# Small norms in a fused five-block kernel: the inverse root moved from ScalarE and VectorE to GpSimd

## The chip, the cores and the metric

The kernel runs on one NeuronCore of one Trainium2 chip. The core has four compute engines with their own instruction queues, which work in parallel and meet only at semaphores: TensorE (PE in the profile; its weight loads are PEld), VectorE (DVE), ScalarE (ACT) and GpSimd (POOL). SyncE (SP) issues most DMA transfers. The metric is the time of one execution on the device, in microseconds (us), as the median of several executions.

## The reference, cut to what matters

A sequence of 256 tokens with 1024 features runs through two layers of one model (a mixer of gated delta rule and mLSTM, then attention with a window; feed-forward parts after each) and two layers of a second one (a mixer of five kinds of attention, then a gated feed-forward part). Everything is float32. Between the large products stand many norms over few numbers, all of this form:

```python
def _rms_norm(x, g):
    xf = x.astype(jnp.float32)
    y = xf * lax.rsqrt(jnp.mean(xf * xf, axis=-1, keepdims=True) + EPS)
    return (y * g.astype(jnp.float32)).astype(x.dtype)

def l2norm(x):
    return x * lax.rsqrt(jnp.sum(x * x, -1, keepdims=True) + EPS)
```

The heads of queries and keys are normed by it one by one, so one norm of 8 heads for 256 tokens has 16 means on each of 128 partitions, and 2 to 32 in the other cases.

## The kernel before

The weights come as float32 and are used as a sum of two halves: for every part of 128x1024 numbers ScalarE writes `weights_high` (L663), VectorE writes `weights_low`, the rest (L765), and TensorE multiplies three times (L490 to L492). Both engines do this for all weights of the kernel, some parts ahead of TensorE, and everything else of theirs is put between by hand: each engine's program is one list in the order in which the code is written (`scalar_program`, `vector_program` and so on), and each instruction waits for the semaphore counts that it needs. A later instruction of an engine never overtakes one that waits.

A small norm went through four engines' queues. GpSimd squares (in the mixer of the second model L2552), VectorE sums (L2378), scales and adds epsilon, and signals `mean` (L2387, L2384, L2480); ScalarE takes the root in place (`scalar_root`, L695) and signals `root`; VectorE takes the reciprocal in place (`vector_inverse`, L784), signals `inverse` and goes on with the product (L2393). There are 21 such roots: one each for the first norm of the input ("ab", tile `inv`), for the l2 norms of the delta rule ("ab l2", L1173), for the two outputs of the first mixer (`ss_b`, `ss_a`) and for the memory (`mem_inv`), and eight in each of the two second-model layers, tile `st`: "memk", "cq", "fox", "mla", "moba", "diff", "memq" and "sub".

The mixer of the second model, `mixer_2`, first projects (2916 columns), with "memk", "cq", "fox" and "mla" between the projections, and then runs six groups of heads through a loop in five stages that are shifted against each other (`skewed`): heads turned into `QK`, scores into `S`, row maximum `mx` and exponentials (L1939), turned probabilities `PT`, values. "moba", "diff" and "memq" prepare the groups 2, 3 and 5 from within that loop, and "sub" norms the output of group 4. ScalarE's place for each root in its list is behind the exponentials of the group before:

```python
    def work(n):
        if n == 2:
            roots("moba", 11, 8)
        elif n == 3:
            roots("diff", 19, 16)
        elif n == 5:
            roots("memq", 35, 4)
```

ScalarE has one table of functions loaded at a time. Where the next function isn't in it, the compiler puts an ACT_TABLE_LOAD ahead of the instruction. Root and exponential are in different tables here; copy, cast and square cause no load. The wide norms over 1024 features (`scalar_sums_root`, L736, with the reciprocal L819) also take their root on ScalarE.

Of the kernel before, what the change touches and what calls it, by code (L numbers as in the profile page):

```python
# [11 lines left out]
ACT = mybir.ActivationFunctionType  # L12
# [3 lines left out]
P = 128  # L16
# [114 lines left out]
class Signal:  # L131
# [18 lines left out]
    def last(self):  # L150
# [3 lines left out]
BY_TENSOR = ["products"]  # L154
BY_SCALAR = ["weight_high", "residual_high", "pair_squares", "turned_high", "squares", "root", "silu", "logs", "decayed", "relu_high", "gated_high",
             "exps", "sink_exps", "trig", "lam_exps"]
BY_VECTOR = ["weight_low", "residual_low", "factored", "mean", "inverse", "diagonal", "residual", "step", "gates", "conv", "spread_gates", "inverse_n",
             "head_mean", "mixed", "angles", "active", "forget", "row_max", "sink_max", "reduced", "normed", "turned",
             "lam", "gated_up", "exp_sums", "minus_sink"]
BY_GPSIMD = ["padding", "pairs_added", "pair_scaled", "l2_squares", "masked", "level_masked", "head_squares", "gained", "relu_square", "k_pair",  # L160
             "feature_squares", "mla_gained", "gate_scaled"]
# [184 lines left out]
def allocate(k, ctx):  # L346
# [410 lines left out]


def vector_split(k, upto):
# [21 lines left out]

def vector_inverse(k, key, x):
    k.V.wait_ge(*k.s.root.at(key))
    k.V.reciprocal(x, x).then_inc(*k.s.inverse(key))  # L784


def vector_rms(k, st, r):
    k.V.wait_ge(*k.s.squares.at((st, NT - 1)))
    k.V.tensor_scalar(r, r, 1.0 / D, EPS, ALU.mult, ALU.add).then_inc(*k.s.mean(st))
    vector_inverse(k, st, r)  # L790

# [377 lines left out]
def scalar_norms_and_values(k):  # L1169
    A, s, m = k.A, k.s, k.ab  # L1170
    yield
    A.wait_ge(*k.banks.was_read("ab l2"))
    A.activation(m.l2, m.l2, ACT.Sqrt).then_inc(*s.root("ab l2"))  # L1173
# [25 lines left out]
def scalar_mixer_ab(k):  # L1199
# [50 lines left out]
    scalar_root(k, "ab b", m.ss_b)  # L1250
# [3 lines left out]
    scalar_root(k, "ab a", m.ss_a)  # L1254
    for k0 in OUT_AB:
# [75 lines left out]
def vector_norms_and_values(k):  # L1331
    V, s, m = k.V, k.s, k.ab
    yield
    V.wait_ge(*s.products.at("ab l2"))
    V.tensor_scalar(m.l2, k.banks["ab l2"][:, 0:16].rearrange("p (t n) -> p t n", t=NT), EPS, None, ALU.add).then_inc(*k.banks.read("ab l2"))
    vector_inverse(k, "ab l2", m.l2)
# [58 lines left out]
def vector_finished(k, name, x, squares, ss, gate):  # L1395
# [14 lines left out]
def vector_mixer_ab(k):  # L1410
# [50 lines left out]
    V.wait_ge(*s.step.last())  # L1461
    V.reciprocal(m.den, m.den).then_inc(*s.inverse("ab den"))
    V.wait_ge(*s.inverse.at("ab den"))
    for t in range(NT):
# [23 lines left out]

def gpsimd_finished(k, name, x, squares, gate, gain, ready):
    G, s = k.G, k.s  # L1490
    for mark in ready:
        G.wait_ge(*mark)
    G.tensor_tensor(squares, x, x, ALU.mult).then_inc(*s.head_squares(name))
    for t in range(NT):
        G.wait_ge(*k.banks.was_read(("ab", COL_Z if name == "a" else COL_O, t)))
    G.tensor_tensor(gate, gate, spread(gain, 1, NT), ALU.mult).then_inc(*s.gained(name))


def gpsimd_mixer_ab(k):
    G, s, m = k.G, k.s, k.ab  # L1500
    G.wait_ge(*s.inputs_landed.at("inputs"))
    gpsimd_rows(k, 0)
    G.memset(m.pad[:, :, :, 0:3], 0.0).then_inc(*s.padding("ab"))
    for c in range(0, 8, 2):
        src = m.flat[:, c * SEQ:(c + 2) * SEQ]
        G.wait_ge(*s.silu.at(c))
        G.tensor_tensor(m.sq[:, c // 2, :], src, src, ALU.mult).then_inc(*s.l2_squares(c))
    causal = k.const("causal3")
    for hd in range(4):
# [23 lines left out]
    G.wait_ge(*s.rows_landed.at(0))  # L1533
    gpsimd_finished(k, "b", m.mixed_b, m.squares_b, m.og, k.row(0, "norm_b"), [k.banks.was_read(("ab h b", t)) for t in range(NT)])
    gpsimd_finished(k, "a", m.mixed_a, m.squares_a, m.zs, k.row(0, "norm_a"), [k.banks.was_read(("ab h a", t)) for t in range(NT)])
    gpsimd_pairs_added(k, ("ab", "post"))
# [769 lines left out]
def scalar_mixer_2(k, l):  # L2306
# [16 lines left out]

    def roots(name, slot, n):
        scalar_root(k, (st, name), m.st[:, :, slot:slot + n])
    projected(0)
    scalar_root(k, (st, "memk"), m.st2[:, :, 12:16])
    projected(512)
    roots("cq", 0, 3)
# [4 lines left out]
    roots("fox", 3, 8)  # L2334
    projected(1536)
# [9 lines left out]
    projected(2048)  # L2345
    scalar_root(k, (st, "mla"), m.st2[:, :, 0:12])
    projected(2560)

    def work(n):
        if n == 2:  # L2350
            roots("moba", 11, 8)
        elif n == 3:
            roots("diff", 19, 16)
        elif n == 5:
            roots("memq", 35, 4)

    def finish(n):
        if n == 4:
            scalar_root(k, (st, "sub"), m.st2[:, :, 0:4])
    scalar_attention(k, k.attention_2[l], work, finish)  # L2360
    for p in range(4):
# [3 lines left out]
def vector_mixer_2(k, l):  # L2365
# [14 lines left out]
    def inverses(name, x, inv):  # L2380
# [7 lines left out]
        vector_inverse(k, (st, name), x)  # L2388
        V.wait_ge(*s.inverse.at((st, name)))
# [90 lines left out]
    V.tensor_scalar(m.st2[:, :, 4:12], m.st2[:, :, 4:12], 1.0 / 64, EPS, ALU.mult, ALU.add).then_inc(*s.mean((st, "mla")))  # L2480
    vector_inverse(k, (st, "mla"), m.st2[:, :, 0:12])
    V.wait_ge(*s.inverse.at((st, "mla")))
# [60 lines left out]
def gpsimd_mixer_2(k, l):  # L2543
# [12 lines left out]
    squared("memk", k.kvm[l][:, :, 0:256], 256, *[k.banks.was_read((("mem", l), 0, t)) for t in range(NT)])  # L2556
    for kind in (*LOW_RANK, FOX):
        squared_columns(*kind)
    squared("mla_q", m.qa, 384, *[k.banks.was_read((st, "qa", t)) for t in range(NT)])
    squared("mla_kv", m.kva, 512, *[k.banks.was_read((st, "kva", t)) for t in range(NT)])  # L2560
    qa4, ka4 = [x.rearrange("p t (n d) -> p t n d", n=4) for x in (m.qa, m.ka)]
    gq, gk = [k.row(2 + l, name).rearrange("p (n d) -> p n d", n=4) for name in ("mla_q", "mla_k")]
    G.wait_ge(*s.normed.at((l, "mla k")))
    for t in range(NT):
        G.tensor_tensor(qa4[:, t], qa4[:, t], gq, ALU.mult).then_inc(*s.mla_gained((l, "q", t)))
        G.tensor_tensor(ka4[:, t, :, 32:96], ka4[:, t, :, 32:96], gk, ALU.mult).then_inc(*s.mla_gained((l, "k", t)))
    for kind in (MOBA, DIFF, MEMQ):
# [165 lines left out]
def gpsimd_program(k):  # L2733
# [137 lines left out]
```

## Time and profile before

| | |
|---|---|
| median of 3 executions | 1685.12 us (1685.05 to 1687.79) |
| the profiled execution | 1684.66 us, span of its instructions 1683.4 us |
| mean granted TensorE clock | 0.939 of full speed |
| PE busy | 1509.1 us, 90% of the span |
| DVE busy | 1075.3 us, 64% |
| ACT busy | 745.0 us, 44% |
| POOL busy | 190.8 us, 11% |

The busy shares are means over stages that differ much. What a wait costs has to be read at its place: which engine works without a pause there, and who stands still until it is done.

### The profile page before, as it was taken

To read this page: it belongs to the slowest core of one execution; us is meant where nothing else is said; L and a number is where in the kernel's file an instruction comes from. 1 tells how busy PE (TensorE), PEld (TensorE's weight loads), DVE (VectorE), ACT (ScalarE), POOL (GpSimd) and SP (SyncE) were. 2 spreads that over 40 slices of the span, in tenths; PEclk is the share of its full clock that TensorE was granted. 3 is DMA by queue.
4 is the path that set the end of the run, shared out by engine and by line. 5 is a ranking of instruction groups with operands and counts; after the bars stand their busy time and mean duration, and the time that the engine had idled before them with its cause. 6 is when DMAs were issued, how large, how long until landed. Compare 5 with 4: busy or idle time off the path is not lost. (4 is left out here: it accounts for less than half of the span.)

```text
span 1683.4 us, 26050 instructions
## 1 busy us (share of the span) xinstructions
PE 1509.1 (90%) x10862; PEld 1422.1 (84%) x10862; DVE 1075.3 (64%) x1533; ACT 745.0 (44%) x1153; POOL 190.8 (11%) x164
## 2 busy tenths in 40 slices
PE   6877987999999787999999869799999958899999
PEld 5865877999997577999997758799998747899999
DVE  4653557665477656764477775577756686677763
ACT  5322324544355444444355534444445544454443
POOL 0002332110000002110011200001001110010100
PEclk9878998999999899999999968899999987899999
DMA  7421203555545214555544410265565420145553
GB/s 234 131 96 50 100 1 126 176 176 188 188 150 174 101 51 148 177 183 193 177 159 142 147 50 26 81 204 184 169 201 182 158 90 1 51 151 176 176 189 112
DMA packets 186389, 230.07 MB, mean 137 GB/s; under 512 B 5920, under 2 KB 161056, under 8 KB 186016
## 3 DMA queue, kind: packets, MB, share of 16 engines
q1 hardware_dynamic: 185264, 221.99, 40.8%
q0 software_dynamic: 1008, 6.41, 1.1%
q8 instruction: 86, 1.41, 0.3%
q14 instruction: 31, 0.25, 0.0%
HBM read 227.34 MB, written 1.05 MB: 136 GB/s over the span
## 5 line engine op out<-in xcount | busy, mean ns | idle before, releaser
L765 DVE TENSOR_TENSOR weights_low<-weights_raw,weights_high 128x1024 fp32r<-128x1024 f32 (+3 forms) x421 | 506.8, 1224 | 352.0 <-ACT weights_high L663 351.5
L663 ACT CAST weights_high<-weights_raw 128x1024 fp32r<-128x1024 f32 (+3 forms) x421 | 424.8, 1030 | 339.9 <-PE bank L492 337.2
L490 PE MATMUL bank<-hT_high,weights_high 128*128 128x256 f32 (+1 forms) x1672 | 488.2, 292 | 39.2 <-DVE hT_low L848 21.5
L491 PE MATMUL bank<-hT_low,weights_high 128*128 128x256 f32 (+1 forms) x1672 | 483.3, 289 | 0.0
L492 PE MATMUL bank<-hT_high,weights_low 128*128 128x256 f32 (+1 forms) x1672 | 482.9, 289 | 0.0
L490 PEld LDWEIGHTS bank<-hT_high,weights_high 128*128 128x128 f32 (+1 forms) x1672 | 330.9, 198 | 46.9 <-issue 30.1
L491 PEld LDWEIGHTS bank<-hT_low,weights_high 128*128 128x128 f32 (+1 forms) x1672 | 330.8, 198 | 0.5
L492 PEld LDWEIGHTS bank<-hT_high,weights_low 128*128 128x128 f32 (+1 forms) x1672 | 330.2, 197 | 0.4
L490 PE MATMUL bank<-aT_high,weights_high 128*128 128x256 f32 x864 | 241.6, 280 | 0.1
L491 PE MATMUL bank<-aT_low,weights_high 128*128 128x256 f32 x864 | 241.6, 280 | 0.0
L492 PE MATMUL bank<-aT_high,weights_low 128*128 128x256 f32 x864 | 240.9, 279 | 0.0
L490 PEld LDWEIGHTS bank<-aT_high,weights_high 128*128 128x128 f32 x864 | 162.4, 188 | 0.5 <-DVE weights_low L765 0.5
L491 PEld LDWEIGHTS bank<-aT_low,weights_high 128*128 128x128 f32 x864 | 162.1, 188 | 0.0
L492 PEld LDWEIGHTS bank<-aT_high,weights_low 128*128 128x128 f32 x864 | 161.7, 187 | 0.0
L490 PE MATMUL bank<-weights_high,hT_high 128*128 128x512 f32 (+1 forms) x288 | 117.6, 408 | 2.4 <-DVE proj L2150 1.8
L492 PE MATMUL bank<-weights_high,hT_low 128*128 128x512 f32 (+1 forms) x288 | 113.6, 394 | 0.0
L491 PE MATMUL bank<-weights_low,hT_high 128*128 128x512 f32 (+1 forms) x288 | 113.5, 394 | 0.0
L1939 ACT ACTIVATE S<-S,mx 128x256 f32<-128x256 f32 (+1 forms) x128 | 57.2, 448 | 102.4 <-DVE mx L2021 80.4
L893 POOL TENSOR_TENSOR pair_sum<-pair_sum,pair_squares 128x512 f32<-128x512 f32 x22 | 31.6, 1438 | 580.6 <-ACT pair_squares L727 497.2
L1871 PE MATMUL bank<-QK 64*128 64x256 f32 (+5 forms) x256 | 46.3, 406 | 24.1 <-issue 23.3
L490 PEld LDWEIGHTS bank<-weights_high,hT_high 128*128 128x128 f32 x288 | 56.6, 196 | 13.3 <-DVE proj L2150 2.0
L492 PEld LDWEIGHTS bank<-weights_high,hT_low 128*128 128x128 f32 x288 | 56.1, 195 | 11.3
(410 smaller groups left out, 1967.5 us busy)
## 6 DMA issues: line engine op xcount, KB each, us to landing
weights_raw<-in_w_up SPq DMA_DIRECT2D x32, 1024.0 KB, 5.3
weights_raw<-in_w_down SPq DMA_DIRECT2D x32, 1024.0 KB, 5.1
weights_raw<-in_ffn_w_gate SPq DMA_DIRECT2D x22, 1024.0 KB, 5.2
weights_raw<-in_ffn_w_up SPq DMA_DIRECT2D x22, 1024.0 KB, 5.2
weights_raw<-in_w_in SPq DMA_DIRECT2D x20, 1024.0 KB, 5.0
weights_raw<-in_w_in_ab SPq DMA_DIRECT2D x16, 1024.0 KB, 5.9
weights_raw<-in_ffn_w_down SPq DMA_DIRECT2D x16, 1024.0 KB, 5.1
weights_raw<-in_w_o SPq DMA_DIRECT2D x10, 1024.0 KB, 4.9
```

Source lines behind the costliest of these rows:

```text
L490: k.E.matmul(out, xh, wh, start=first, stop=False)
L491: k.E.matmul(out, xh, wl, start=False, stop=False)
L492: return k.E.matmul(out, xl, wh, start=False, stop=last)
L663: k.A.copy(w.halves(n)[0], w.raw_part(n)).then_inc(*k.s.weight_high(n))
L765: k.V.tensor_tensor(low, w.raw_part(n), high.bitcast(F32), ALU.subtract).then_inc(*k.s.weight_low(n))
L893: k.G.tensor_tensor(k.acc[:, :], k.acc[:, :], k.sq[:, p % 2, :], ALU.add).then_inc(*k.s.pairs_added((st, p)))
L1871: mm = E.matmul(bank[:, x * nk:(x + 1) * nk], m.QK[i][p0:p0 + d, c, t * P:(t + 1) * P], m.QK[i][p0:p0 + d, g.key_block(c), 0:nk], start=Tr ...
L1939: e = A.activation(m.S[:, i, hh, c0:c0 + nk], m.S[:, i, hh, c0:c0 + nk], ACT.Exp, bias=m.mx[:, i, t, hh:hh + 1], accum_out=m.den[:, i, t, ...
```

## The change

All 21 small roots and their reciprocals go. In their place GpSimd raises the mean to the power minus one half, in place, with one two-operand instruction whose second operand is a column that holds -0.5, spread over the shape (`gpsimd_inverse`). VectorE's `mean` is what GpSimd waits for, and `inverse` is now signalled by GpSimd. VectorE waits for `inverse` where it waited before, except for the norms "ab", "ab l2" and "mem": there the reciprocal stood in VectorE's list, and now nothing stands in its place. The wide norms keep ScalarE's root. The core of the diff:

```diff
+def gpsimd_inverse(k, key, x):
+
+    k.G.wait_ge(*k.s.mean.at(key))
+    k.G.tensor_tensor(x, x, minus_half(k, x), ALU.pow).then_inc(*k.s.inverse(key))
...
-def scalar_root(k, key, x):
-    k.A.wait_ge(*k.s.mean.at(key))
-    k.A.activation(x, x, ACT.Sqrt).then_inc(*k.s.root(key))
...
-def vector_inverse(k, key, x):
-    k.V.wait_ge(*k.s.root.at(key))
-    k.V.reciprocal(x, x).then_inc(*k.s.inverse(key))
...
 def gpsimd_finished(...):
     G.tensor_tensor(gate, gate, spread(gain, 1, NT), ALU.mult).then_inc(*s.gained(name))
+    gpsimd_inverse(k, "ab " + name, ss)
...
 def gpsimd_mixer_2(k, l):
     squared("memk", k.kvm[l][:, :, 0:256], 256, ...)
-    for kind in (*LOW_RANK, FOX):
+    gpsimd_inverse(k, (st, "memk"), m.st2[:, :, 12:16])
+    for kind in LOW_RANK:
         squared_columns(*kind)
+    gpsimd_inverse(k, (st, "cq"), m.st[:, :, 0:3])
+    squared_columns(*FOX)
+    gpsimd_inverse(k, (st, "fox"), m.st[:, :, 3:11])
     squared("mla_q", ...)
     squared("mla_kv", ...)
+    gpsimd_inverse(k, (st, "mla"), m.st2[:, :, 0:12])
...
     for kind in (MOBA, DIFF, MEMQ):
         squared_columns(*kind)
+    gpsimd_inverse(k, (st, "moba"), m.st[:, :, 11:19])
+    gpsimd_inverse(k, (st, "diff"), m.st[:, :, 19:35])
+    gpsimd_inverse(k, (st, "memq"), m.st[:, :, 35:39])
+    gpsimd_inverse(k, (st, "sub"), m.st2[:, :, 0:4])
     gpsimd_pairs_added(k, ("ff2", l))
```

The line numbers of the changed kernel differ from those before; names and tiles are the same. ScalarE's list in the attention loop of the first `mixer_2`, from the heads of group 0 to the exponentials of group 2, was:

```order
L1922 COPY QK<-bank 128x512
L1939 ACT_TABLE_LOAD
L1939 ACTIVATE S,den<-S,mx 128x128 x4
L1939 ACTIVATE S,den<-S,mx 128x256 x4
L1922 COPY QK<-bank 96x512 x2
L695 ACT_TABLE_LOAD
L695 ACTIVATE st<-st 128x2x8
L1955 COPY PT<-bank 128x512 x2
L1939 ACT_TABLE_LOAD
L1939 ACTIVATE S,den<-S,mx 128x128 x4
L1939 ACTIVATE S,den<-S,mx 128x256 x4
```

and is now, at the same place:

```order
L1924 COPY QK<-bank 128x512
L1941 ACTIVATE S,den<-S,mx 128x128 x4
L1941 ACTIVATE S,den<-S,mx 128x256 x4
L1924 COPY QK<-bank 96x512 x2
L1957 COPY PT<-bank 128x512 x2
L1941 ACTIVATE S,den<-S,mx 128x128 x4
L1941 ACTIVATE S,den<-S,mx 128x256 x4
```

The root of "moba" and three table loads are gone from it. Over the kernel 50 table loads become 31.

GpSimd's list in the same mixer, from the last squares to the additions for the next norm, has the powers of "moba", "diff", "memq" and "sub" behind the squares of all heads; before, it had none of the rows with `minus_half`:

```order
L2535 TENSOR_TENSOR pair_squares<-hp 128x1024
L2535 TENSOR_TENSOR squares<-hp 128x1024
L2535 TENSOR_TENSOR pair_squares<-hp 128x512
L762 TENSOR_TENSOR st<-st,minus_half 128x2x8
L762 TENSOR_TENSOR st<-st,minus_half 128x2x16
L762 TENSOR_TENSOR st<-st,minus_half 128x2x4 x2
L895 TENSOR_TENSOR pair_sum<-pair_sum,pair_squares 128x512 x2
```

Three wide norms get a table load that they didn't have, because the table of the root was still there from a small norm: the one behind the first mixer ("post", below) and the first one of the feed-forward part in each layer of the second model. ScalarE's list ahead of "post" ended so before:

```order
L727 ACTIVATE pair_squares<-bank 128x512 x3
L663 CAST weights_high<-weights_raw 128x1024 x2
L736 ACTIVATE post_factor<-bank,consts 128x256
```

and ends so now, with the load between the casts and the root:

```order
L722 ACTIVATE pair_squares<-bank 128x512 x3
L664 CAST weights_high<-weights_raw 128x1024 x2
L731 ACT_TABLE_LOAD
L731 ACTIVATE post_factor<-bank,consts 128x256
```

## Rows read from the trace of the kernel before

**Rows 1.** Busy time in four stretches: us, busy (instructions) of each engine, clock, DMA
```profile
core 0: us, PE busy (x) PEld busy (x) DVE busy (x) ACT busy (x) POOL busy (x), PEclk, DMA share, GB/s
892.00:955.00 63.00, 61.09 (x272) 48.75 (x273) 44.56 (x67) 34.74 (x47) 6.92 (x6) 1.00 0.46 155
965.00:1065.00 100.00, 75.26 (x488) 67.94 (x488) 67.79 (x129) 46.56 (x131) 2.58 (x2) 0.78 0.13 43
1100.00:1287.00 187.00, 186.93 (x1550) 185.96 (x1549) 133.40 (x177) 82.92 (x101) 17.12 (x14) 1.00 0.58 185
1350.00:1460.00 110.00, 81.46 (x541) 73.39 (x539) 77.11 (x148) 51.69 (x138) 8.23 (x7) 0.83 0.13 46
```

**Rows 2.** The reciprocals, line L784: ns min/median/max, start, forms; idle before them
```profile
L784 DVE RECIPROCAL st<-st x16: 191/230/354, 904.9 to 1459.5; 128x8 f32<-128x8 f32 x6, 128x16 f32<-128x16 f32 x4, 128x6 f32<-128x6 f32 x2, 128x24 f32<-128x24 f32 x2
...
  ACT st L695: 24.1, 16
```

**Rows 3.** Groups of ScalarE instructions: count, busy us, mean ns, idle before
```profile
L695 ACT ACT_TABLE_LOAD x12 | 15.4, 1283 | 0.2
...
L1939 ACT ACT_TABLE_LOAD x9 | 11.5, 1283 | 0.2
```

**Rows 4.** VectorE's timeline: start, length, instruction, [idle before it <-releaser]
```profile
957.30 0.30 DVE L784 RECIPROCAL st<-st 128x24 f32<-128x24 f32 x1 [0.29 <-ACT st L695]
...
986.58 0.25 DVE L784 RECIPROCAL st<-st 128x16 f32<-128x16 f32 x1 [2.88 <-ACT st L695]
...
1001.73 0.35 DVE L784 RECIPROCAL st<-st 128x32 f32<-128x32 f32 x1 [3.65 <-ACT st L695]
...
1028.26 0.20 DVE L784 RECIPROCAL st<-st 128x8 f32<-128x8 f32 x1 [3.80 <-ACT st L695]
...
1063.76 0.20 DVE L784 RECIPROCAL st<-st 128x8 f32<-128x8 f32 x1 [0.28 <-ACT st L695]
...
1382.14 0.26 DVE L784 RECIPROCAL st<-st 128x16 f32<-128x16 f32 x1 [3.55 <-ACT st L695]
```

**Rows 5.** TensorE's timeline behind "moba", first layer
```profile
991.39 1.09 PE L498 MATMUL bank<-consts,hp 128*128 128x128 f32 x8 [2.77 <-DVE hp L923]
```

**Rows 6.** ScalarE's timeline at "moba", first layer
```profile
985.04 1.28 ACT L695 ACT_TABLE_LOAD   x1
986.33 0.22 ACT L695 ACTIVATE st<-st 128x16 f32<-128x16 f32 x1
```

**Rows 7.** VectorE's timeline behind "memq", first layer
```profile
1031.23 0.69 DVE L775 TENSOR_TENSOR hT_low<-bank,hT_high 128x512 fp32r<-128x512 f32 x1 [1.31 <-ACT hT_high L674]
```

**Rows 8.** Groups of GpSimd instructions by shape
```profile
L2552 POOL TENSOR_TENSOR pair_squares<-hp 128x512 f32<-128x512 f32 x2 | 2.1, 1040 | 15.7 <-DVE st L2378 15.7
...
L2552 POOL TENSOR_TENSOR pair_squares<-hp 128x64 f32<-128x64 f32 x2 | 0.6, 294 | 20.1 <-DVE st L2378 20.1
```

**Rows 9.** Timeline of VectorE and GpSimd: one hands over to the other
```profile
244.71 0.68 DVE L1476 COPY scratch<-bank 128x512 f32<-128x512 f32 x1
...
245.54 1.90 POOL L1493 TENSOR_TENSOR scratch<-scratch 128x1024 f32<-128x1024 f32 x1 [5.33 <-DVE scratch L1476]
```

**Rows 10.** Timeline at the norm `ss_b`
```profile
237.87 2.35 POOL L1496 TENSOR_TENSOR both_gates<-both_gates,rows 128x1024 f32<-128x1024 f32 x1
...
242.07 0.20 DVE L784 RECIPROCAL ss_b<-ss_b 128x8 f32<-128x8 f32 x1 [1.83 <-ACT ss_b L695]
...
244.85 0.99 PE L498 MATMUL bank<-consts,qkv 128*128 128x128 f32 x7 [1.33 <-DVE qkv L1407]
```

**Rows 11.** Timeline of the wide norm "post" behind the first mixer
```profile
275.16 0.47 ACT L736 ACTIVATE post_factor<-bank,consts 128x256 f32<-128x256 f32 x1 [0.19 <-PE bank L640]
...
276.33 1.75 DVE L819 RECIPROCAL post_factor<-post_factor 128x256 f32<-128x256 f32 x1
```

**Rows 12.** Timeline at the norm "ab", start of the kernel
```profile
15.16 1.28 ACT L695 ACT_TABLE_LOAD   x1
...
16.69 0.17 DVE L784 RECIPROCAL inv<-inv 128x2 f32<-128x2 f32 x1 [0.67 <-ACT inv L695]
...
17.22 0.39 PE L490 MATMUL bank<-hT_high,weights_high 128*16 128x256 f32 x1 [5.24 <-DVE weights_low L765]
```

More of the change, by code:

```diff
@@ L154 @@
 BY_TENSOR = ["products"]
-BY_SCALAR = ["weight_high", "residual_high", "pair_squares", "turned_high", "squares", "root", "silu", "logs", "decayed", "relu_high", "gated_high",
+BY_SCALAR = ["weight_high", "residual_high", "pair_squares", "turned_high", "squares", "silu", "logs", "decayed", "relu_high", "gated_high",
              "exps", "sink_exps", "trig", "lam_exps"]
-BY_VECTOR = ["weight_low", "residual_low", "factored", "mean", "inverse", "diagonal", "residual", "step", "gates", "conv", "spread_gates", "inverse_n",
+BY_VECTOR = ["weight_low", "residual_low", "factored", "mean", "diagonal", "residual", "step", "gates", "conv", "spread_gates", "inverse_n",
              "head_mean", "mixed", "angles", "active", "forget", "row_max", "sink_max", "reduced", "normed", "turned",
              "lam", "gated_up", "exp_sums", "minus_sink"]
-BY_GPSIMD = ["padding", "pairs_added", "pair_scaled", "l2_squares", "masked", "level_masked", "head_squares", "gained", "relu_square", "k_pair",
+BY_GPSIMD = ["padding", "inverse", "pairs_added", "pair_scaled", "l2_squares", "masked", "level_masked", "head_squares", "gained", "relu_square", "k_pair",
              "feature_squares", "mla_gained", "gate_scaled"]
@@ L377, in allocate @@
     k.junk = k.sq[:, :, :].rearrange("p k n -> p (k n)")
+    k.half = sbuf("minus_half", [P, 1])[:, :]
     width, n_raw, n_half = 8 * 256, 3, 2
@@ L754, in scalar_residual, with minus_half @@
         scalar_pair_square(k, st, p, src.rearrange("p k n -> p (k n)"))
+def minus_half(k, x):
+    return k.half.to_broadcast(list(x.shape)) if len(x.shape) == 2 else spread(spread(k.half, 1, x.shape[1]), 2, x.shape[2])[:, :, :, 0]
+def gpsimd_inverse(k, key, x):
+    k.G.wait_ge(*k.s.mean.at(key))
+    k.G.tensor_tensor(x, x, minus_half(k, x), ALU.pow).then_inc(*k.s.inverse(key))
 def vector_split(k, upto):
@@ L1171, in scalar_norms_and_values @@
     yield
-    A.wait_ge(*k.banks.was_read("ab l2"))
-    A.activation(m.l2, m.l2, ACT.Sqrt).then_inc(*s.root("ab l2"))
     yield
@@ L1249, in scalar_mixer_ab @@
         A.copy(m.U[:, j, :], k.banks[key][:, :]).then_inc(*k.banks.read(key))
-    scalar_root(k, "ab b", m.ss_b)
     A.wait_ge(*s.products.at(("ab h a", 0)))
@@ L1253, in scalar_mixer_ab @@
     scalar_feature_major(k, "ab b", 4, [v[:, 4:8, :] for v in m.top])
-    scalar_root(k, "ab a", m.ss_a)
     for k0 in OUT_AB:
@@ L1461, in vector_mixer_ab @@
     V.wait_ge(*s.step.last())
-    V.reciprocal(m.den, m.den).then_inc(*s.inverse("ab den"))
-    V.wait_ge(*s.inverse.at("ab den"))
+    V.reciprocal(m.den, m.den).then_inc(*s.step())
+    V.wait_ge(*s.step.last())
     for t in range(NT):
@@ L1486, in vector_mixer_ab, with gpsimd_finished @@
     vector_add_post(k, "ab", m, ("ff1", 0), k.hT, ff1_gain(k, 0))
-def gpsimd_finished(k, name, x, squares, gate, gain, ready):
+def gpsimd_finished(k, name, x, squares, ss, gate, gain, ready):
     G, s = k.G, k.s
@@ L1502, in gpsimd_mixer_ab @@
     gpsimd_rows(k, 0)
+    G.memset(k.half, -0.5)
     G.memset(m.pad[:, :, :, 0:3], 0.0).then_inc(*s.padding("ab"))
+    G.wait_ge(*s.padding.at("ab"))
+    gpsimd_inverse(k, "ab", m.inv)
     for c in range(0, 8, 2):
@@ L1507, in gpsimd_mixer_ab @@
         G.tensor_tensor(m.sq[:, c // 2, :], src, src, ALU.mult).then_inc(*s.l2_squares(c))
+    G.wait_ge(*k.banks.was_read("ab l2"))
+    G.tensor_tensor(m.l2, m.l2, minus_half(k, m.l2), ALU.pow).then_inc(*s.inverse("ab l2"))
     causal = k.const("causal3")
@@ L1533, in gpsimd_mixer_ab @@
     G.wait_ge(*s.rows_landed.at(0))
-    gpsimd_finished(k, "b", m.mixed_b, m.squares_b, m.og, k.row(0, "norm_b"), [k.banks.was_read(("ab h b", t)) for t in range(NT)])
-    gpsimd_finished(k, "a", m.mixed_a, m.squares_a, m.zs, k.row(0, "norm_a"), [k.banks.was_read(("ab h a", t)) for t in range(NT)])
+    gpsimd_finished(k, "b", m.mixed_b, m.squares_b, m.ss_b, m.og, k.row(0, "norm_b"), [k.banks.was_read(("ab h b", t)) for t in range(NT)])
+    gpsimd_finished(k, "a", m.mixed_a, m.squares_a, m.ss_a, m.zs, k.row(0, "norm_a"), [k.banks.was_read(("ab h a", t)) for t in range(NT)])
     gpsimd_pairs_added(k, ("ab", "post"))
@@ L2322, in projected @@
         scalar_token_linear(k, st, ("in_2", l), n0, evacuate, side)
-    def roots(name, slot, n):
-        scalar_root(k, (st, name), m.st[:, :, slot:slot + n])
     projected(0)
-    scalar_root(k, (st, "memk"), m.st2[:, :, 12:16])
     projected(512)
-    roots("cq", 0, 3)
     projected(1024)
@@ L2333, in scalar_mixer_2 @@
         A.copy(m.cT[:, i, :], k.banks[st, "cT", i][:, 0:SEQ]).then_inc(*k.banks.read((st, "cT", i)))
-    roots("fox", 3, 8)
     projected(1536)
@@ L2345, in scalar_mixer_2 @@
     projected(2048)
-    scalar_root(k, (st, "mla"), m.st2[:, :, 0:12])
     projected(2560)
[L2349 to L2360, printed above, removed]
+    scalar_attention(k, k.attention_2[l])
     for p in range(4):
@@ L2480, in vector_mixer_2 @@
     V.tensor_scalar(m.st2[:, :, 4:12], m.st2[:, :, 4:12], 1.0 / 64, EPS, ALU.mult, ALU.add).then_inc(*s.mean((st, "mla")))
-    vector_inverse(k, (st, "mla"), m.st2[:, :, 0:12])
     V.wait_ge(*s.inverse.at((st, "mla")))
@@ L2741, in gpsimd_program @@
     gpsimd_memory(k)
+    gpsimd_inverse(k, "mem", k.mem.inv)
     gpsimd_mixer_c(k)
```

5 lines of the change are left out of this document (removed).

## The prediction

> **What bounds the kernel now.** I read the busy time by stretch first. In the projections of the second model's mixer TensorE is busy 61.09 of 63 us, in the feed-forward part 186.93 of 187 us [rows 1]. There nothing on another engine can cost or save time unless it grows past that cover. In the two attention loops TensorE is busy only 75.26 of 100 and 81.46 of 110 us, at a granted clock of 0.78 and 0.83, and VectorE 67.79 and 77.11 us: no engine is full, so waits between engines set the time. Then I read what VectorE waits for ahead of the reciprocals. All 16 on tile `st` together stand behind 24.1 us of idle VectorE, every one of them released by ScalarE's root [rows 2]. The timeline at "moba" shows why: the heads' mean ended at 983.70, but ScalarE was still in exponentials and then loaded a table for 1.28 us at 985.04, ahead of a root of 0.22 us [rows 4, 6]. Last I asked at each place who waits for VectorE. Behind "moba" TensorE had stood still 2.77 us for the rotated heads `hp` [rows 5]: the wait is on the path. Behind "memq" VectorE stands still again, 1.31 us, for a cast of ScalarE that was waiting for TensorE's products [rows 7]: that wait is not.
>
> **What goes.** From end of mean to end of reciprocal is idle plus reciprocal [rows 4]. First layer: mla 0.29 + 0.30 = 0.59; moba 2.88 + 0.25 = 3.13; diff 3.65 + 0.35 = 4.00; sub 0.28 + 0.20 = 0.48; sum 8.20 us. Second layer: moba 3.55 + 0.26 = 3.81 in place of 3.13, the others alike to 0.1 us, so 8.88. Together 17.08 us. "memq" has 3.80 + 0.20 = 4.00, but its saving is a longer wait at 1031.23, so I count 0; were it all to come through I would be 4 us a layer too high. "memk", "cq" and "fox" lie among the projections, under TensorE's 61.09 of 63 us: 0 as well; without that cover each would give or cost what mla does. The 12 table loads ahead of the roots and 9 ahead of exponentials take 1283 ns each [rows 3], but those are ScalarE's time. The former count inside the waits above, and the latter ran while ScalarE would have waited for row maxima anyway, so I add nothing for them.
>
> **What comes instead.** No row shows a power. GpSimd's multiplies take 294 ns for 64 columns and 1040 ns for 512 [rows 8]: 746 ns / 448 = 1.66 ns a column and 0.19 us fixed. The hand-over from VectorE to GpSimd is 245.54 - (244.71 + 0.68) = 0.15 us [rows 9]; the way back I take as the 0.03 us from the end of a root (986.33 + 0.22) to VectorE's start at 986.58 [rows 4, 6]. So a site costs 0.19 + 0.14 + 0.03 = 0.36 us, plus c for each column. With 24, 16, 32 and 8 columns in mla, moba, diff and sub there are 80 columns on the path in a layer. The eight sites save 17.08 - 8 x 0.36 = 14.20 us, minus 160 c.
>
> c decides the sign. Its lower end is the multiply's 1.66 ns, as if a power were one step. Its upper end I take as 60 to 90 such steps, 100 to 150 ns, because a power is a logarithm, a product and an exponential, computed on an engine whose loops I can price only by its multiply. The nearest row is the multiply's, but I don't take it: I choose 50 ns, some 30 multiplies. At 50 ns: moba costs 0.36 + 0.80 = 1.16 (saves 1.97, 2.65 in the second layer), diff 0.36 + 1.60 = 1.96 (saves 2.04), mla 1.56 (loses 0.97), sub 0.76 (loses 0.28). Sum 2.76 + 3.44 = 6.20 us.
>
> The Trainium skill ("GPSIMD Engine Reference", Performance pitfalls for Q7 kernels and Specifications) gives 4 cycles of 1.2 GHz for each step of a dependent chain in fp32. If a power is such a chain of 25 to 30 steps without overlap, that is an estimate of 83 to 100 ns a column and nearly no gain; no row here shows such a chain.
>
> **The four other places.** (1) Start. Root and load go, and VectorE's idle 0.67 us and reciprocal 0.17 us stood between it and the first `weights_low`, for which TensorE had waited 5.24 us [rows 12]: it starts 0.84 us earlier, in a stretch that it then bounds; I count 0.85. If the transfers bind there soon after, it is 0. The power itself is needed much later. (2) `ss_b`. Idle 1.83 + reciprocal 0.20 = 2.03 us; GpSimd's own product ends at 237.87 + 2.35 = 240.22, just as the mean does, so the power costs 0.36 + 8 c = 0.76 us. The saving is 1.27; TensorE's idle of 1.33 us there [rows 10] is its cap. `ss_a` and "ab l2" stand beside other waits of VectorE and count 0 (within 0.3 us). (3) "post" gets a table load it did not have: 1.28 us, of which ScalarE's idle 0.19 hides some, so the root ends 1.09 later, at 275.16 + 0.47 + 1.09 = 276.72, and the reciprocal starts at 276.77 in place of 276.33 [rows 11]: 0.44 us lost. (4) The two feed-forward parts get such a load too, some 1.3 us on ScalarE, which is busy only 82.92 of 187 us under a TensorE without a gap [rows 1]: 0. Were the cover gone, it would be 1.3 us a layer.
>
> **Sum.** 6.20 + 0.85 + 1.27 - 0.44 = 7.88 us. The profiled execution, 1684.66 us with a span of 1683.4, becomes 1676.8; it is 0.46 below the median of the runs, so the median becomes 1677.2. In general the gain is 14.20 + 0.85 + 1.67 - 0.44 = 16.28 us minus 168 c. At 1.66 ns the cap at `ss_b` takes 0.3 of it: 15.7 us, 1669.4. At 97 ns it is nothing, at 150 ns a loss of 8.9 us, 1694.0. A measurement of this kernel can tell about 0.2%, 3.4 us, from no change: faster below c = 77 ns, slower above 117 ns.
>
> The other rule is on the table loads: the Trainium skill ("ScalarE: Activation LUTs", What ACT_TABLE_LOAD costs) adds a drain to the load and comes to about 2.66 us for a switch. The row shows the load at 985.04 and the root at 986.33, so 1.30 us in all; the drain is not seen in this case [rows 6], and by the page the saving at each site could only be larger than what I count.
>
> **The rivals.**
> - *The power is slow* (the other side). Mechanism: GpSimd takes over 117 ns a column, VectorE stands behind it at mla, moba, diff and sub (80 columns a layer), and the wait for a power of diff alone would be 0.36 + 32 x 0.15 = 5.16 us at 150 ns, against 4.00 now. For it: the engine is the slowest with plain products, 1.04 us for 512 columns. Against it: 64 multiplies' worth of time a column is much. 1694, chance 0.24; 1691 at 132 ns.
> - *Saved waits are taken up by TensorE*, at moba and diff as at memq [rows 7]. Then only the losses at mla and sub (2 x 1.25), start, `ss_b` and "post" stay: -2.50 + 0.85 + 1.27 - 0.44 = -0.8, that is 1685.9, no change. Against it stands the 2.77 us for which TensorE waited on VectorE behind moba [rows 5]. Chance 0.12.
> - *The power is nearly as cheap as a multiply*, c under 20 ns: 1669.4 to 1672.2. For it speaks that the nearest row is the multiply's. Chance 0.16.
> - *TensorE's clock moves with it.* In the attention loops it is granted 0.78 and 0.83 of full speed, with 1.00 where TensorE has no gap [rows 1]: of its two levels, 1.2 and 2.4 GHz, the lower one holds a good part of these loops. Shorter gaps may bring it back to the higher one. One tenth more in both loops, on 75.26 + 81.46 us of busy TensorE, of which I judge a fifth to be on the path, is some 3 us: 1674. The opposite is as well possible, 1680. Chance 0.11, all within faster.
> - *It doesn't do what it says*: the order of the changed kernel shows roots, reciprocals and 19 table loads gone. No chance.
>
> **How the numbers follow.** The likeliest case, c between 20 and 77 ns with the savings as counted, has 0.37 and gives 1677.2, with 1671 to 1682 as its own range. Faster: 0.37 + 0.16 + 0.11 minus 0.02, which I put to a c near break-even with losses elsewhere = 0.62. Same: 0.12 for the absorbed waits and 0.03 for such a c = 0.15. Slower: 0.23. For the range, cheap powers go down to 1669.4; I put the lower end at 1668 for a clock that helps as well. Upwards it takes in the absorbed case and the slow power up to 132 ns: 1691. What is left out is c above that, about 0.16, and some 0.04 below.
>
> **What would show it.** The power's duration on `st` at 8, 16, 24 and 32 columns gives 0.19 us + c at once, and VectorE's idle ahead of the heads' product should be that plus 0.17 us: 1.16 at moba, 1.96 at diff. TensorE's wait behind moba should fall from 2.77 to about 0.8 us; VectorE's wait at 1031.23 should grow by what memq saves. ScalarE should have no table load within the loops, and one ahead of the root of "post", whose reciprocal comes 0.4 us later against the mean. The prediction is wrong if c is off by a factor of two, if a power has a fixed cost well above 0.19 us (each 1 us of it is 9 us), or if the clock of the loops differs by more than 0.05.

## The result and the profile after

| | kernel before | changed kernel |
|---|---|---|
| median | 1684.32 us (1680.66 to 1688.21, 17 runs) | 1692.30 us (1686.86 to 1694.83, 17 runs) |
| ratio | | 1.0042, 95% interval 1.0033 to 1.0052 |
| profiled execution, span | 1683.4 us | 1690.1 us |

The changed kernel is slower by 0.42%, some 7 us (the two medians are 8.0 us apart), where 1677.2 us and a gain had been forecast. 1692.3 lies above the range, which ended at 1691. It ended on the side of the rival "the power is slow".

First the page's busy times of the changed kernel (us, share, number of instructions). Against the table of the kernel before ScalarE has 27 us less, VectorE 4 us less and GpSimd 52 us more:

```profile
PE 1506.8 (89%) x10862; PEld 1414.6 (84%) x10862; DVE 1071.4 (63%) x1512; ACT 718.0 (42%) x1113; POOL 242.5 (14%) x186
```

The powers by shape, from the groups of GpSimd instructions (count, busy us, mean ns, then the idle time before them):

```profile
L762 POOL TENSOR_TENSOR st<-st,minus_half 128x16 f32<-128x16 f32 x4 | 11.6, 2898 | 32.7 <-DVE st L2372 32.7
L762 POOL TENSOR_TENSOR st<-st,minus_half 128x32 f32<-128x32 f32 x2 | 10.8, 5416 | 22.6 <-DVE st L2372 22.6
L762 POOL TENSOR_TENSOR st<-st,minus_half 128x8 f32<-128x8 f32 x6 | 9.9, 1646 | 148.9 <-DVE st L2369 104.0 <-DVE st L2372 44.9
L762 POOL TENSOR_TENSOR st<-st,minus_half 128x24 f32<-128x24 f32 x2 | 8.3, 4153 | 29.6 <-DVE st L2464 29.6
...
L762 POOL TENSOR_TENSOR inv<-inv,minus_half 128x2 f32<-128x2 f32 x1 | 0.7, 717 | 6.7 <-DVE inv L792 6.7
```

From 16 to 32 columns 5416 - 2898 = 2518 ns are added, 157 ns for each; what is left, 2898 - 16 x 157 = 386 ns, is fixed. I had 50 ns and 0.19 us.

VectorE's timeline, first second-model layer, the rows that answer to [rows 4]. The product stands now directly behind the wait:

```profile
955.34 0.43 DVE L2466 TENSOR_TENSOR qa<-qa,st 128x256 f32<-128x256 f32 x1 [4.27 <-POOL st L762]
...
983.69 1.22 DVE L2377 TENSOR_TENSOR hp<-hp,st 128x1024 f32<-128x1024 f32 x1 [3.01 <-POOL st L762]
...
1000.43 1.23 DVE L2377 TENSOR_TENSOR hp<-hp,st 128x1024 f32<-128x1024 f32 x1 [5.53 <-POOL st L762]
...
1024.54 0.69 DVE L2377 TENSOR_TENSOR hp<-hp,st 128x512 f32<-128x512 f32 x1 [1.75 <-POOL st L762]
1029.70 0.69 DVE L783 TENSOR_TENSOR hT_low<-bank,hT_high 128x512 fp32r<-128x512 f32 x1 [3.74 <-ACT hT_high L675]
1063.64 0.76 DVE L2512 TENSOR_TENSOR gb<-gb,st 128x256 f32<-128x256 f32 x2 [1.75 <-POOL st L762]
```

Before, from the end of a mean to the start of the product (idle, reciprocal, and 0.04 us behind it), it was 0.63 us at mla, 3.17 at moba, 4.04 at diff, 0.52 at sub. So mla lost 4.27 - 0.63 = 3.64 us, moba won 0.16 (0.84 in the second layer, where it had 3.85), diff lost 1.49, sub lost 1.23. That is 6.20 us in the first layer and 5.52 in the second. At memq the wait fell from 4.04 to 1.75 us, and the wait at 1029.70, which had been 1.31 us in [rows 7], grew to 3.74: the 2.3 us are given back to 0.1.

TensorE's timeline at moba. It waits 0.45 us for the heads, in [rows 5] it was 2.77. VectorE's product starts 4.52 us ahead of it as before (983.69 and 988.21; 986.87 and 991.39), but TensorE's own work ahead of it ends later against that product, at 984.41 + 3.35 = 987.76. So the wait had shrunk although VectorE was only 0.16 us faster there, and the sign that I had told readers to look for would have misled them:

```profile
984.41 3.35 PE L1873 MATMUL bank<-QK 96*128 96x128 f32 x16
988.21 1.10 PE L499 MATMUL bank<-consts,hp 128*128 128x128 f32 x8 [0.45 <-DVE hp L925]
```

Both engines at the four places outside the attention loops, which answer to [rows 10 to 12]: start, `ss_b`, `ss_a`, and "post" with its new table load.

```profile
16.06 0.39 PE L491 MATMUL bank<-hT_high,weights_high 128*16 128x256 f32 x1 [4.29 <-DVE weights_low L773]
...
237.88 1.23 DVE L1400 TENSOR_TENSOR qkv<-qkv,ss_b 128x1024 f32<-128x1024 f32 x1 [1.75 <-POOL ss_b L762]
...
247.12 1.23 DVE L1400 TENSOR_TENSOR scratch<-scratch,ss_a 128x1024 f32<-128x1024 f32 x1 [1.75 <-POOL ss_a L762]
...
270.26 1.28 ACT L731 ACT_TABLE_LOAD   x1
271.55 0.47 ACT L731 ACTIVATE post_factor<-bank,consts 128x256 f32<-128x256 f32 x1
```

TensorE starts 1.16 us earlier; its wait shrank by 0.95 (5.24 to 4.29), and the other 0.2 us this execution was ahead already before the norm. ss_b wins 2.07 - 1.75 = 0.3 us; ss_a, which I had counted as nothing, waits 1.75 us for its power, and VectorE fell back there by 1.2 us against the kernel before. Behind the new load of "post" the root ends at 272.02, and VectorE, which had not waited for it before, waits 0.37 us.

### The profile page after: what moved, and what is told of

It is laid out like the page before. It is cut to its first block and busy times, and to the rows that moved or that the text cites. A ratio compares the mean times of both kernels' runs of the same rounds, so it can differ in the third digit from the quotient of the medians.

```text
span 1690.1 us, 26012 instructions
## 1 busy us (share of the span) xinstructions
PE 1506.8 (89%) x10862; PEld 1414.6 (84%) x10862; DVE 1071.4 (63%) x1512; ACT 718.0 (42%) x1113; POOL 242.5 (14%) x186
## 5 line engine op out<-in xcount | busy, mean ns | idle before, releaser
L491 PEld LDWEIGHTS bank<-hT_high,weights_high 128*128 128x128 f32 (+1 forms) x1672 | 325.6, 195 | 50.5 <-issue 34.6
L492 PEld LDWEIGHTS bank<-hT_low,weights_high 128*128 128x128 f32 (+1 forms) x1672 | 325.8, 195 | 0.5
L493 PEld LDWEIGHTS bank<-hT_high,weights_low 128*128 128x128 f32 (+1 forms) x1672 | 325.2, 195 | 0.4
L762 POOL TENSOR_TENSOR st<-st,minus_half 128x8 f32<-128x8 f32 (+4 forms) x16 | 43.2, 2703 | 235.3 <-DVE st L2369 104.0
L1873 PE MATMUL bank<-QK 64*128 64x256 f32 (+5 forms) x256 | 50.9, 442 | 29.2 <-issue 28.3
L1873 PEld LDWEIGHTS bank<-QK 64*128 64x128 f32 (+2 forms) x256 | 37.4, 249 | 38.1 <-issue 31.5
```

Of the source, the lines that this page charges most:

```text
L491: k.E.matmul(out, xh, wh, start=first, stop=False)
L492: k.E.matmul(out, xh, wl, start=False, stop=False)
L493: return k.E.matmul(out, xl, wh, start=False, stop=last)
L762: k.G.tensor_tensor(x, x, minus_half(k, x), ALU.pow).then_inc(*k.s.inverse(key))
L1873: mm = E.matmul(bank[:, x * nk:(x + 1) * nk], m.QK[i][p0:p0 + d, c, t * P:(t + 1) * P], m.QK[i][p0:p0 + d, g.key_block(c), 0:nk], start=Tr ...
```

## The experiments

Executions of one kernel spread over 2 to 19 us, mostly 5 to 10, so a ratio is good to some 0.14 to 0.24%, and to 0.34% for the kernel with the widest spread (the one that keeps the root at sub and ss_a). Kernels that mix both ways have a list of the norms whose power is on GpSimd; all others take ScalarE's root and VectorE's reciprocal at their old places in the lists:

```diff
+ON_GPSIMD = (...)
+def on_gpsimd(key):
+    return (key[1] if isinstance(key, tuple) else key) in ON_GPSIMD
 def scalar_root(k, key, x):
+    if not on_gpsimd(key):
         k.A.wait_ge(*k.s.mean.at(key))
         k.A.activation(x, x, ACT.Sqrt).then_inc(*k.s.root(key))
```

**1. Where the change costs.** The first run has the power at five norms outside the second model's mixer, the second at the 16 within it.

```diff
+ON_GPSIMD = ('ab', 'ab l2', 'ab b', 'ab a', 'mem')
```

> Power on GpSimd only for the five sites outside the second model's mixer (ab, ab l2, ss_b, ss_a, mem); the 16 sites on st as before. Theory A (the 8.3 us by which the changed kernel's profile was ahead at 868 us come from these five sites): about 1676 to 1679 us. Theory B (they are mostly the spread of executions; the sum by the measured power is start -0.85, ss_b +0.2 less nothing, ss_a +1.2, post +0.44): 1684 to 1685 us, no change to tell.

Measured: 1676.90 us, ratio 0.9959 (0.9942 to 0.9977). That was theory A's number, and it didn't last: experiment 5 below takes most of it away from the powers.

```diff
+ON_GPSIMD = ('memk', 'cq', 'fox', 'mla', 'moba', 'diff', 'memq', 'sub')
```

> Power on GpSimd only for the 16 sites on st; the other five as before. Sum of the waits at mla, moba, diff and sub with the measured durations, mean to product: first layer +3.64 -0.16 +1.49 +1.23 = 6.2 us, second +3.64 -0.84 +1.49 +1.23 = 5.5 us, so 11.7 us in all, 1696 us. Theory A wants more, some 1698 (8 us a layer less what is hidden); theory B expects it close to the changed kernel or up to 11.7 us above the kernel before.

Measured: 1690.84 us, ratio 1.0047 (1.0030 to 1.0064). The loss is in the 16: 7.9 us against the kernel before, where the waits give 11.7, and 14 us against the control of experiment 5 (1.0047 / 0.9963).

**2. The same kernel with a cheap instruction.** A multiply in place of each power; the factors of the norms are then means times 0.01, not inverse roots.

```diff
-    k.G.tensor_tensor(x, x, minus_half(k, x), ALU.pow).then_inc(*k.s.inverse(key))
+    k.G.tensor_tensor(x, x, minus_half(k, x), ALU.mult).then_inc(*k.s.inverse(key))
```

> The changed kernel with a multiply by a constant in place of each power (the inverses are not roots, so the values are others; every instruction, wait and place is the same but for the operation). If the duration of the power is what the prediction got wrong and its frame of waits holds, the gain of my sum for 1.66 ns a column appears: 15.7 us, about 1669 us. Rival (waits saved at moba and diff are taken up by TensorE): about 1684 us minus the start and ss_b, 1682.

Measured: 1656.53 us, ratio 0.9840 (0.9821 to 0.9859), 27 us below the kernel before. The groups of GpSimd instructions and VectorE's timeline of this run:

```profile
L787 POOL TENSOR_TENSOR st<-st,minus_half 128x8 f32<-128x8 f32 x6 | 1.2, 204 | 141.4 <-DVE st L2420 100.7 <-DVE st L2423 40.8
...
L787 POOL TENSOR_TENSOR st<-st,minus_half 128x32 f32<-128x32 f32 x2 | 0.5, 242 | 22.6 <-DVE st L2423 22.6
```
```profile
977.29 1.22 DVE L2429 TENSOR_TENSOR hp<-hp,st 128x1024 f32<-128x1024 f32 x1 [0.33 <-POOL st L787]
...
988.86 1.23 DVE L2429 TENSOR_TENSOR hp<-hp,st 128x1024 f32<-128x1024 f32 x1 [0.36 <-POOL st L787]
```

The multiply takes 204 ns for 8 columns and 242 for 32, 1.6 ns a column and 0.19 us fixed, and the whole hand-over is 0.33 to 0.36 us. By the prediction's 0.36 us a site and 1.66 ns a column the hand-over would be 0.39 us at moba and 0.41 at diff, so that price was right to 0.06 us; what was priced wrongly is the power itself, which has twice the multiply's fixed part and a hundred times its slope. The gain is larger than the 15.7 us of my sum.

**3. Is memq behind the extra gain?** As experiment 2, but memq keeps its root.

> The run with a multiply in place of every power (1656.5 us; the inverses have other values), but memq keeps its root on ScalarE and reciprocal on VectorE. My prediction's step 'memq saves nothing, TensorE's products absorb it': 1656.5 us, no difference. Theory C (once moba and diff save their waits, TensorE keeps its full clock into the output products, and memq's wait of some 4 us a layer is on the path): 1656.5 + 8 = 1664 us.

Measured: 1657.95 us, ratio 0.9849 (0.9828 to 0.9870), against 0.9840: no difference to tell. Theory C fell. VectorE's timeline of this run shows the wait back at memq:

```profile
1013.90 0.20 DVE L780 RECIPROCAL st<-st 128x8 f32<-128x8 f32 x1 [3.81 <-ACT st L774]
...
1050.49 0.69 DVE L808 TENSOR_TENSOR hT_low<-bank,hT_high 128x512 fp32r<-128x512 f32 x1 [1.34 <-ACT hT_high L675]
```

The last row stands behind sub. In the run without the root the same instruction stands at 1049.53, 0.96 us earlier; but that much it was ahead already at moba (977.29 against 978.25). The 3.8 us are absorbed before it, and the row that answers to [rows 7] shows where: without the root VectorE waits there, with the root it doesn't.

```profile
1012.99 0.69 DVE L808 TENSOR_TENSOR hT_low<-bank,hT_high 128x512 fp32r<-128x512 f32 x1 [2.13 <-ACT hT_high L675]
```

That is what the prediction had said of memq.

**4. Only the hidden and short ones.**

```diff
+ON_GPSIMD = ('ab', 'ab l2', 'ab b', 'mem', 'memq')
```

> Power on GpSimd only where it is short or hidden: ab, ab l2, ss_b, mem and memq. Start gains 0.85 us, ss_b 2.03 - 1.81 = 0.2 us, post keeps its table because the root of ss_a is still ahead of it. Theory B: 1683 us, within 0.2% of the kernel before. Theory A: about 1677 us.

Measured: 1675.12 us, ratio 0.9947 (0.9929 to 0.9965). That is theory A's side again (1677), but 9 us are far more than the traces show for so few norms. So I tested what all these kernels have in common.

**5. The control: no power at all, only the leftovers.** Besides the lines shown, the reciprocal of the first mixer's denominator signals another semaphore, as in the changed kernel.

```diff
+ON_GPSIMD = ()
     k.junk = k.sq[:, :, :].rearrange("p k n -> p (k n)")
+    k.half = sbuf("minus_half", [P, 1])[:, :]
...
+    G.memset(k.half, -0.5)
```

> No power anywhere: the kernel before, with only the memset of the column minus_half left on GpSimd and the reciprocal of the first mixer's denominator signalled by another semaphore. If the 6.9 us of the run with five powers come from those powers: 1683 to 1685 us. If they come from these small leftovers, or from the chip's and the day's spread: about 1677 us.

Measured: 1679.32 us, ratio 0.9963 (0.9949 to 0.9977). 5 us come without any power. Three kernels took the leftovers apart. The kernel before with one unused column:

> The kernel before with nothing but one more column of 4 bytes a partition allocated, never written or read: all buffers allocated after it lie 4 bytes further. If the control's 5 us come from where the buffers lie: 1679 us. If not: 1684 us.

Measured: 1679.35 us, ratio 0.9966 (0.9952 to 0.9980). The kernel before itself, under another name:

> The kernel before, unchanged, under another name. It should give 1684 us, ratio 1.000; if it is off by 3 us or more, the comparison itself moves by as much, and the control's 5 us are no effect of its edits.

Measured: 1684.06 us, ratio 0.9997 (0.9980 to 1.0013). The semaphore of the denominator's reciprocal:

```diff
-    V.reciprocal(m.den, m.den).then_inc(*s.inverse("ab den"))
-    V.wait_ge(*s.inverse.at("ab den"))
+    V.reciprocal(m.den, m.den).then_inc(*s.step())
+    V.wait_ge(*s.step.last())
```

> The kernel before, only the reciprocal of the first mixer's denominator signals the semaphore step in place of inverse. One wait of VectorE on itself either way: 1684 us. If the control's 5 us come from this: 1679 us.

Measured: 1685.22 us, ratio 1.0001 (0.9985 to 1.0018). So it is the 4-byte column, which nobody reads: the buffers allocated behind it, weights and activations among them, lie 4 bytes further. How it acts is taken up in the next experiment.

**6. How far the shift goes.** The column 8 and 16 wide in the kernel before, and 16 wide in the changed one.

```diff
-    k.half = sbuf("minus_half", [P, 1])[:, :]
+    k.half = sbuf("minus_half", [P, 16])[:, 0:1]
```

> The kernel before with 32 unused bytes a partition. If what counts is the place within 32 bytes: 1684 us; if within 64: another time than 1684 us, in either direction.

Measured: 1678.15 us, ratio 0.9964 (0.9945 to 0.9983).

> The kernel before with 64 unused bytes a partition in place of 4. If what counts is where a buffer lies within 64 bytes: 1684 us as before. If any shift helps: 1679 us.

Measured: 1672.45 us, ratio 0.9933 (0.9915 to 0.9951). With a period of 32 or 64 bytes these two kernels would have been back at 1684 us; neither is. Of the four places the last is the best.

> The changed kernel with minus_half 16 columns wide (64 bytes a partition, the first used), so that the buffers behind it keep their place within 64 bytes as in the kernel before. If the powers cost what their durations say (11.7 to 13 us) and the 4-byte shift had hidden 4.5 us of it: 1696 to 1697 us. If the placement doesn't matter to this kernel: 1692 us.

Measured: 1683.15 us, ratio 0.9982 (0.9968 to 0.9996). My expectation was 13 us off, because it rested on that period. What the run is good for is a comparison at equal placement: the change costs 1.0042 / 0.9966 = 1.0076 with 4 bytes in both, 12.8 us (about 3 us either way, from the two intervals), and 0.9982 / 0.9933 = 1.0049 with 64 bytes in both, 8.3 us (about 4 either way; the two medians are 10.7 us apart). The waits read above sum to 11.7 us; the places outside the loops nearly cancel.

Where the placement acts can be read from a stretch around the first feed-forward part in which TensorE is hardly ever short of work and its clock is full, 310 to 470 us, in the kernel before, with 4 bytes and with 64 bytes (columns as in [rows 1]):

```profile
310.00:470.00 160.00, 160.00 (x1350) 160.00 (x1349) 89.39 (x90) 68.75 (x76) 18.25 (x16) 1.00 0.59 189
```
```profile
310.00:470.00 160.00, 160.00 (x1359) 160.00 (x1358) 89.93 (x90) 68.94 (x75) 18.28 (x16) 1.00 0.60 190
```
```profile
310.00:470.00 160.00, 159.18 (x1366) 158.62 (x1365) 92.14 (x92) 68.69 (x76) 19.93 (x17) 1.00 0.60 193
```

1350, 1359 and 1366 products in the same 160 us. But the kernels don't stand at the same work there: with 64 bytes this part starts 6.0 us earlier, and the end of the stretch already holds the next stage, with TensorE's gap. It is cleaner to take the time of the same products. All traces have 10862 of them, in the same order, and this is what the start times give (us; in brackets how many of them TensorE was at 1.2 GHz):

| | before | copy | 4 bytes | 32 bytes | 64 bytes |
|---|---|---|---|---|---|
| 582 products within the first up projection | 69.84 | 69.84 | 68.87 | 68.87 | 65.96 |
| the same, ns from start to start | 120.0 | 120.0 | 118.3 | 118.3 | 113.3 |
| 679 products within the first down projection | 79.97 | 79.97 | 79.97 | 79.97 | 79.97 |
| VectorE's product at diff to that at sub, first layer | 61.9 (18.2) | 61.8 (18.1) | 57.8 (10.0) | 57.8 (10.0) | 60.6 (17.3) |
| the same, second layer | 62.0 (15.2) | 62.1 (15.2) | 61.8 (18.3) | 60.8 (17.1) | 61.8 (15.2) |

So the placement acts in two ways. It changes the pace of TensorE in some parts (the up projection) and not in others (the down projection). And it changes how long TensorE is granted only 1.2 GHz in the attention loops: with 4 bytes the largest single piece of the gain, 4.1 us, lies behind diff in the first layer, where 10.0 us at 1.2 GHz stand in place of 18.2, while the pace gives 1.0 us in the first up projection. Why either follows from where the buffers lie isn't shown. The column isn't alone in it, either: in two runs of experiment 7 with the same 4 bytes (the early means with ScalarE's roots, and the version that keeps them at sub and ss_a) 714 products within the second down projection take 80.92 us, in all others 84.09.

This also says what the comparisons at equal placement are worth. From diff to sub in the first layer the changed kernel needs 63.2 us with 4 bytes and 58.8 with 64. Against its partner that is 5.5 us more and 1.8 us less, where the wait at sub accounts for 1.2 us more in both, and memq's for nothing. So the clock has its share of some 4 us in the 12.8 and of 3 us, the other way, in the 8.3, an estimate from these rows. Against the kernel before itself TensorE's products from ahead of mla to behind sub take 5.1 us longer in the first layer and 4.8 in the second, 9.9 us in all.

**7. The power under cover.** If its duration on the path is the cost, forming the mean earlier must hide it. VectorE's list is changed so that the means of moba and diff are formed ahead of the attention loop, memq's right behind its squares, and mla's ahead of the next projection:

```diff
     projected(2560)
     squared(MOBA)
+    averaged_early(MOBA)
+    squared(DIFF)
+    averaged_early(DIFF)
 
     def work(n):
         if n == 2:
             scaled(MOBA)
             turned_heads("moba", C_MOBA, 8, 64, ROT_M, ROT_C + ROT_A)
-            squared(DIFF)
             squared(MEMQ)
+            averaged_early(MEMQ)
```

> The changed kernel, all powers on GpSimd, but VectorE forms the means of mla, moba, diff and memq earlier in its own list, so that the power runs while VectorE works on other things. If the duration of the power on the path is what costs: against the changed kernel's 1692.3 it saves per layer 3.6 (mla), 3.0 (moba), 5.5 (diff), so 24 us, 1668 us; with the clock's share and memq as in the multiply's run another 5 to 8 us, 1661 us. If GpSimd's long instructions cost in another way (a shared resource slowing VectorE): well above 1675 us.

Measured: 1664.31 us, ratio 0.9878 (0.9859 to 0.9896). GpSimd's timeline of this run shows moba's and diff's powers, 8.28 us together, beside other work of VectorE; in that loop VectorE waits for no power but that of sub:

```profile
967.30 8.28 POOL L787 TENSOR_TENSOR st<-st,minus_half 128x16 f32<-128x16 f32 x2
...
982.76 1.64 POOL L787 TENSOR_TENSOR st<-st,minus_half 128x8 f32<-128x8 f32 x1 [7.18 <-DVE st L2423]
```

The earlier means alone, with ScalarE's roots where they were. The edit moves the mean of mla too, which the expectation doesn't name:

> The kernel before with moba's, diff's and memq's means formed earlier, roots still on ScalarE at their old places in its list. If ScalarE's list and its table loads are what VectorE waits for, the earlier mean gives nothing: 1683 us. If the late mean was a part of the wait: 1676 us or less.

Measured: 1676.50 us, ratio 0.9963 (0.9946 to 0.9980), the same as the control's 0.9963. From diff to sub this run needs 57.8 and 61.9 us, as the control does. So the earlier mean by itself gives nothing that can be told from the spread. The two have to go together: an engine that is free at that time, and a mean that is early.

The version to which all this points keeps ScalarE's root at sub and ss_a, whose power nothing covers:

```diff
-ON_GPSIMD = ('ab', 'ab l2', 'ab b', 'ab a', 'mem', 'memk', 'cq', 'fox', 'mla', 'moba', 'diff', 'memq', 'sub')
+ON_GPSIMD = ('ab', 'ab l2', 'ab b', 'mem', 'memk', 'cq', 'fox', 'mla', 'moba', 'diff', 'memq')
```

> The run with early means (1664.3 us), but sub and ss_a, whose power stands on the path without cover, keep ScalarE's root. Saved: 1.75 - 0.48 = 1.2 us twice at sub, 1.75 - 0.2 = up to 1.2 us at ss_a if its root is not waited for, and the added table load of post, 0.4 us: 1660.5 us. If the table loads that come back in the loop delay the exponentials: 1664 us or more.

Measured: 1652.83 us (1646.44 to 1664.98), ratio 0.9816 (0.9782 to 0.9850), the fastest with 4 bytes. VectorE's wait at sub is 0.28 us again:

```profile
1046.32 0.20 DVE L780 RECIPROCAL st<-st 128x8 f32<-128x8 f32 x1 [0.28 <-ACT st L774]
```

With 64 bytes:

> The run with early means and sub and ss_a on ScalarE (1652.8 us), with 64 bytes in place of 4. If the placement's 4.5 us add to the rest: 1657.5 us. If they don't: 1653 us.

Measured: 1650.00 us, ratio 0.9797 (0.9773 to 0.9821): 34 us below the kernel before, though its interval overlaps that of the run with 4 bytes, so that it isn't shown that the placement adds. Its expectation still rested on the period of 64 bytes.

## Why the prediction was wrong, step by step

- **The step that failed** is "I choose 50 ns, some 30 multiplies" in the part on what comes instead: the power's c was 157 ns, and its fixed part 0.39 us, not 0.19. Of my bounds (1.66 to 150 ns) even the upper one was a little too low. That a power is a logarithm, a product and an exponential on this engine, from which I had that upper bound, no run shows. With the measured numbers the same sum gives 16.28 - 168 x 0.157 = -10.1 us, and 9 x 0.2 = 1.8 us of fixed cost more, so 11.9 us slower. That is the 11.7 us of the waits, and within the intervals at both equal placements (12.8 and 8.3 us). The length of a stage confirms the wait in it: from moba's product to diff's the kernel before took 15.25 us, the changed one 16.74 in both layers, 1.49 us more, which is the wait lost at diff. So it is the rival "the power is slow", given 0.24, that came true. The frame of the sum held; one price in it was off by three. (The hand-over is 0.15 us where it was read and 0.14 in the sum; for nine sites that is 0.1 us.)
- **The rule that spoke against the change.** By the Trainium skill ("GPSIMD Engine Reference", Performance pitfalls for Q7 kernels and Specifications) a dependent step takes 4 cycles at 1.2 GHz; 157 ns a column would be 47 such steps, an estimate. By that rule I had 83 to 100 ns, nearer to the measured 157 than my 50, so it had the right direction; no run here shows how a power is built.
- **mla** was the worst place, 3.64 us a layer: 24 columns in one power, and before it had waited only 0.29 us for ScalarE, which had nothing else to do there. **moba** came out even, **diff** lost 1.5, **sub** 1.2.
- **memq saves nothing**: right in both directions, 2.3 us in the changed kernel and 3.8 us in experiment 3 are given back.
- **The table loads** went as the order showed, and those ahead of the exponentials gave nothing, as I had said: from moba's product to diff's the kernel with the multiply is 3.69 us shorter than the control (11.57 and 15.26), and the wait at diff alone fell by 3.68 (4.04 to 0.36). The rival that TensorE takes up the saved waits at moba and diff is false: with the multiply both waits fell to 0.33 and 0.36 us and the kernel gained more than the sum.
- **Start**: 0.95 us against my 0.85. **ss_b**: 0.3 against 1.27, for the power's price alone. **ss_a** was mis-sized: I put its root beside other waits, and with a power of 1.63 us VectorE falls back 1.2 us. **"post"** has its load, and VectorE waits 0.37 us for its root, where I had 0.44.
- **The clock.** From mla's product to sub's in the second layer TensorE was at 1.2 GHz for 51.4 of 108.3 us, where it had been 37.6 of 106.5. The granted clock there fell from 0.82 to 0.76, one of the signs that I had named. It cost nothing beyond the waits, though: the stage grew by 1.83 us, and its waits by 1.88 (moba, diff and sub).
- **What I had no term for** is the placement: the diff adds a column of 4 bytes, and that alone gives -0.34% (0.9966, 0.9952 to 0.9980). Without the control I would have read the 7 us as the price of the powers, which is 8 to 13 us, and the run with five powers (-6.9 us) as a proof that those five pay. Its ratio, 0.9959, is that of the control, 0.9963, within the intervals; the one of experiment 4, 0.9947, isn't clear of it. That the measured time came so close to the upper end of my range, 1691, is owed in part to this column and not to the sum, which gives 1697 with the measured prices.
- **Open** is why the multiply gains 22.8 us against the control where my sum has 15.7. From mla's product to diff's it wins 7.2 us in the first layer and 6.9 in the second, which the sum has nearly; behind that, between diff's product and sub's, another 1.2 and 5.2 us appear. In the second layer TensorE is at 1.2 GHz for 10.2 us of that stretch in place of 18.4, in the first for 10.0 us in both. That fits the rival on TensorE's clock, but no run separates it. Open in part is why the version with ScalarE's root at sub and ss_a gains 11 us over the run with early means, where 4 were expected: the two profiled executions are only 2.9 us apart, and 3.2 us of gain stand in the second down projection (84.09 and 80.92 us), for which I have no cause. Open, too, is which rule of addresses stands behind the placement.

## What to carry to other kernels

Before an operation is moved to another engine, price it there by itself, with its shape: a multiply's row says nothing about a power's (here 1.6 against 157 ns a column). A slow instruction on an engine that is free cost nothing here at moba, diff and memq once its input was ready early enough, and forming the means earlier turned a loss of 8 us into a gain of 20 (against the control, a loss of 13 into a gain of 15). And a change that adds a buffer, even an unused one, needs a control that adds only the buffer. To see where two kernels differ, compare the time between the same two instructions; a fixed window of time holds different work in each.

## What the runs showed that I had not expected

- GpSimd's two-operand power takes 0.39 us + 157 ns for each column of 128 float32; its multiply at the same shapes 0.19 us + 1.6 ns.
- The place of the buffers changes the pace of back-to-back float32 products at full granted clock in some parts: 120.0, 118.3 and 113.3 ns from start to start in the first up projection with 0, 4 and 64 bytes ahead of the buffers, and 117.8 ns in the first down projection with all three. The kernel takes 1684, 1679 and 1672 us (1678 with 32 bytes), and a part of that is TensorE's granted clock in the attention loops.
- ScalarE's table load was again 1.28 us and the root of "post" started 0.01 us behind it, 270.26 + 1.28 against 271.55. The Trainium skill ("ScalarE: Activation LUTs", What ACT_TABLE_LOAD costs) adds a drain of about the same length again; it is not seen in this kernel, where ScalarE's instruction before the load of "post" ends 0.02 us ahead of it.
